# A two-block transformer kernel on one core: the first norm in wide pieces on three engines, parameter rows loaded behind it, the last norm applied while banks are emptied, one weight split moved among norm jobs

## The chip, the cores and the metric

The kernel runs on one core of one Trainium2 chip. The metric is the device time of one execution in microseconds (us), the smaller the better. The kernel before took 2709.87 us (median of 3 runs, 2707.84 to 2711.51).

Engine names in rows: PE is TensorE (matmul), PEld its weight load, DVE is VectorE, ACT is ScalarE, POOL is GpSimd, SP is SyncE. A name with a q behind it (ACTq, SPq, PEq) is the instruction queue of that engine: issuing a DMA is shown there.

## The reference, cut to what matters

Sequence 256, width 1024, two blocks of two layers each, everything in float32. Only the places that the change touches are written out.

```
def rmsnorm(x, g):                         # gain g per column
    return x * rsqrt(mean(x*x, -1) + 1e-6) * g

# block 1, layer 0 begins
h    = rmsnorm(x, g_mix[0])                # the FIRST norm
proj = h @ w_in[0]                         # first weights used: the 512 columns of a_in ("glu")
# ... three attentions, a convolution, gates, w_out, a convolutional FFN; then layer 1

# block 2, layer l: xs (256 rows of latents), cs (256 rows of context), both modulated
xs, cs = ffn_half_step(xs, ..), ffn_half_step(cs, ..)
hx = rmsnorm(xs, mix_norm[l]) * (1 + m1) + m0
hc = rmsnorm(cs, mix_norm[l]) * (1 + n1) + n0
px = hx @ w_in[l]                          # "in": 4 units of 256 columns, then q, kv, k_rope
# in the last layer hc is needed for the kv columns only
# ... latent attention, Fourier mix, convolution, w_out, a second FFN
return rmsnorm(xs, final_norm)             # the LAST norm, behind the last FFN
```

## The kernel before, in words

Activations lie transposed in SBUF: `x[128, 8, 256]` holds chunk c of 128 model columns on the partitions and the 256 tokens along the row. A matrix product is done in float32 quality out of three products of a rounded format: every operand is split into a high part and a rest, and PE computes high·high, rest·high and high·rest (lines 917 to 919). So each weight tile goes through one pipeline, called a *unit* here (up to 128 x 2048 numbers, 1 MB): SP loads it into one of four slots of `raw` (line 761), ACT rounds it into `whi` (`copy`, line 1378), DVE subtracts to get `wlo` (line 1842), and PE runs 48 matmuls of 256 columns per unit. Semaphores count units: `s_raw` landed, `s_hi` rounded, `s_lo` rest ready, `s_acc` matmuls done, `s_accfree` bank emptied. A slot of `raw` is free once the rest of the unit in it is computed. Every engine runs its own list of instructions strictly in the order in which it is written out by hand; there is no scheduler.

A norm over the 1024 columns (`norm_x`) works like this. ACT squares the eight chunks of x into `sq` (line 1424). DVE adds seven of them into `rstd` (lines 1873, 1875). PE multiplies a matrix of ones with that sum and with the eighth square, so that each partition of `stat` holds the sum over all columns (lines 876, 878). DVE transposes `stat` into `root` (line 1885), ACT takes the root of a few columns (`few`, line 1452), DVE inverts them (1893) and spreads them back into `rstd` (1895). Then come *jobs*, one per chunk: DVE writes `hf = x·gain·rstd` (1920), ACT rounds it into `h_hi`, DVE subtracts to get `h_lo` (1905, or 1907 with a bias). The gain is a column of `par`.

**The head.** All small parameters (gains, biases, convolution taps) lie in HBM as rows. 65 small DMAs fetch them into `prow`, every second one issued by ACT (line 1375), the others by POOL (line 800), and PE turns the seven blocks of 128 rows into columns of `par` (line 864, evacuated by ACT, 1378). ACT issues the load of x (1372), of the constant tables (1373) and its half of the rows first, and only then begins to compute: it copies the turned x out of four banks, rounds the first unit, squares. DVE waits for all of `par` before it goes on with the norm (the wait in front of line 2072). PE turns the rows between the norm's sums and the first matmuls of "glu" (`first_units`, 939 to 941).

**"in" of the last layer.** `scale_norm` on DVE runs 16 jobs, the eight of xs first, then the eight of xc. Units 0 and 1 of "in" are used by PE while the jobs of xs are made. ACT rounds unit 2 and DVE makes its rest only after all 16 jobs. A unit's result goes out of its bank by ACT (`fr`, `cb`, `u`), the last one by DVE (line 2335), and the next phase, q01, may begin once all of these banks are emptied.

**The tail.** After the last unit of the last FFN (`down1`, eight units, one per chunk of x), DVE adds the gated result to x (2281), ACT squares it, PE sums, DVE and ACT make `rstd`, DVE makes eight tiles `fin = x·gain·rstd` (1915), PE turns them back in sixteen 128x128 transposes (864), ACT copies four banks into `ostage` (1378), and SP writes 1 MB to HBM in one DMA (791).

## Time and profile before

| | |
|---|---|
| median of 3 runs | 2709.87 us |
| the profiled execution | 2706.84 us |
| its span (first to last instruction) | 2705.0 us |
| PE busy | 2578.7 us, 95% of the span |
| PE weight load busy | 2252.0 us, 83% |
| DVE busy | 1482.9 us, 55% |
| ACT busy | 1035.0 us, 38% |
| POOL busy | 76.4 us, 3% |
| chain that ended last | PE 87%, DVE 6%, ACT 3%, issue 2%, POOL 1%, DVEq 1% |
| mean granted TensorE clock | 0.991 of full |

The span is what the profile sees; the execution's own time is 1.84 us more. "Busy" for PE counts overlapping, pipelined matmuls. The granted clock has two levels here, 1.2 and 2.4 GHz; 0.50 in a window means that the whole window ran at 1.2 GHz.

### The profile page before, as it was taken

What the parts mean: (1) busy time and instruction counts of PE and PEld (TensorE: products, weight loads), DVE (VectorE), ACT (ScalarE), POOL (GpSimd) and SP (SyncE); (2) the same over time, 40 slices, a digit from 0 to 9 for tenths busy, and PEclk for the clock granted to TensorE, in tenths of its full rate; (3) what the DMA queues carried; (4) which work ended last, traced back from release to release, by engine and by line L of the source; (5) the groups of instructions that cost most, each with busy time, mean ns of one, the idle gap of its engine ahead of it and who ended that gap; (6) DMA issues with size and microseconds to landing.
All of it is one profiled execution on the core that took longest, in us unless ns stands there. A gap on an engine that the chain in (4) does not pass through costs nothing.

```text
span 2705.0 us, 47365 instructions
## 1 busy us (share of the span) xinstructions
PE 2578.7 (95%) x19887; PEld 2252.0 (83%) x19887; DVE 1482.9 (55%) x2170; ACT 1035.0 (38%) x1411; POOL 76.4 (3%) x108
## 2 busy tenths in 40 slices
PE   6998999999899999999999999999999999898998
PEld 5998999899889978888776678888788888776998
DVE  4787786787678563333525564333543333546555
ACT  4445464555456432122334432122332222444433
POOL 4003000000200000000000000000000000000000
PEclk9999999999999999999999999999999999999999
DMA  7477765757676552432426542332342433554572
GB/s 207 162 251 165 210 181 161 220 193 228 162 213 172 166 161 80 115 95 74 158 79 196 157 125 79 103 107 72 119 129 75 120 88 92 164 164 132 152 204 91
DMA packets 613576, 393.61 MB, mean 146 GB/s; under 512 B 47804, under 2 KB 609656, under 8 KB 613270
## 3 DMA queue, kind: packets, MB, share of 16 engines
q1 hardware_dynamic: 609552, 383.03, 48.7%
q0 software_dynamic: 2816, 6.53, 1.2%
q8 instruction: 136, 2.23, 0.4%
q10 hardware_dynamic: 1029, 1.47, 0.1%
q14 instruction: 43, 0.34, 0.0%
HBM read 389.94 MB, written 1.05 MB: 145 GB/s over the span
## 4 chain that ended last, share of the span: by engine, by line
PE 87%; DVE 6%; ACT 3%; issue 2%; POOL 1%; DVEq 1%; ACTq 0%; POOLq 0%
PE acc L917 12%; PE acc L918 12%; PE acc L919 12%; PE scores L917 6%; PE scores L918 6%; PE scores L919 6%; PE scores L958 3%; PE scores L960 3%; PE scores L959 3%; PE acc L958 3%; PE acc L960 3%; PE acc L959 3%; DVE wlo L1842 2%; PE stat L1085 2%; ACT whi L1378 1%
## 5 line engine op out<-in xcount | busy, mean ns | idle before, releaser
L1378 ACT ACTIVATE whi<-raw 128x2048 fp32r<-128x2048 f32 (+2 forms) x336 | 567.5, 1690 | 848.1 <-PE acc L919 236.3
L1842 DVE TENSOR_TENSOR wlo<-raw,whi 128x2048 fp32r<-128x2048 f32 (+2 forms) x315 | 653.5, 2075 | 245.4 <-ACT whi L1378 244.9
L917 PE MATMUL acc<-h_hi,whi 128*128 128x256 f32 (+1 forms) x2084 | 671.6, 322 | 19.8 <-DVE x L2217 7.8
L918 PE MATMUL acc<-h_lo,whi 128*128 128x256 f32 (+1 forms) x2084 | 663.3, 318 | 0.0
L919 PE MATMUL acc<-h_hi,wlo 128*128 128x256 f32 (+1 forms) x2084 | 662.6, 318 | 0.0
L917 PEld LDWEIGHTS acc<-h_hi,whi 128*128 128x128 f32 x2084 | 395.7, 190 | 58.1 <-DVE wlo L1842 13.6
L918 PEld LDWEIGHTS acc<-h_lo,whi 128*128 128x128 f32 x2084 | 396.1, 190 | 28.4 <-issue 1.2
L919 PEld LDWEIGHTS acc<-h_hi,wlo 128*128 128x128 f32 x2084 | 396.0, 190 | 27.5
L917 PE MATMUL scores<-h_hi,whi 128*128 128x256 f32 (+1 forms) x928 | 310.6, 335 | 0.1
L918 PE MATMUL scores<-h_lo,whi 128*128 128x256 f32 (+1 forms) x928 | 309.0, 333 | 0.0
L919 PE MATMUL scores<-h_hi,wlo 128*128 128x256 f32 (+1 forms) x928 | 309.0, 333 | 0.0
L917 PEld LDWEIGHTS scores<-h_hi,whi 128*128 128x128 f32 x928 | 174.9, 188 | 20.4 <-issue 1.4
L918 PEld LDWEIGHTS scores<-h_lo,whi 128*128 128x128 f32 x928 | 175.0, 189 | 17.4
L919 PEld LDWEIGHTS scores<-h_hi,wlo 128*128 128x128 f32 x928 | 175.0, 189 | 17.4
L958 PE MATMUL scores<-a_hi,whi 128*128 128x256 f32 (+1 forms) x528 | 177.8, 337 | 4.3 <-DVE wlo L1842 4.3
L958 PE MATMUL acc<-a_hi,whi 128*128 128x256 f32 (+1 forms) x528 | 177.1, 335 | 1.3 <-DVE wlo L1842 1.3
L959 PE MATMUL scores<-a_lo,whi 128*128 128x256 f32 (+1 forms) x528 | 177.4, 336 | 0.0
L960 PE MATMUL scores<-a_hi,wlo 128*128 128x256 f32 (+1 forms) x528 | 177.4, 336 | 0.0
L959 PE MATMUL acc<-a_lo,whi 128*128 128x256 f32 (+1 forms) x528 | 176.8, 335 | 0.0
L960 PE MATMUL acc<-a_hi,wlo 128*128 128x256 f32 (+1 forms) x528 | 176.6, 335 | 0.0
L2306 DVE TENSOR_TENSOR a_hi<-sg,acc 128x512 f32 (+3 forms) x48 | 29.8, 621 | 238.9 <-PE acc L919 238.9
L2306 DVE TENSOR_TENSOR a_hi<-sg,scores 128x512 f32 (+3 forms) x40 | 24.8, 621 | 191.3 <-PE scores L919 191.3
(302 smaller groups left out, 3487.8 us busy)
## 6 DMA issues: line engine op xcount, KB each, us to landing
raw<-in_ffn_w_in_dram SPq DMA_DIRECT2D x176, 512.0 KB, 5.0
raw<-in_w_mod_dram SPq DMA_DIRECT2D x72, 1024.0 KB, 5.2
raw<-in_w_in_dram SPq DMA_DIRECT2D x62, 1024.0 KB, 5.8
raw<-in_w_up_dram SPq DMA_DIRECT2D x88, 512.0 KB, 5.1
raw<-in_ffn_w_out_dram SPq DMA_DIRECT2D x64, 704.0 KB, 4.7
raw<-in_w_down_dram SPq DMA_DIRECT2D x32, 704.0 KB, 4.8
raw<-in_w_out_dram SPq DMA_DIRECT2D x16, 1024.0 KB, 5.9
raw<-in_w_branch_dram SPq DMA_DIRECT2D x16, 512.0 KB, 6.9
```

Source lines behind the costliest of these rows:

```text
L917: pe.matmul(bank, wh, hi[:, c0 + k, 0:width], start=(k == 0), stop=False)
L918: pe.matmul(bank, wh, lo[:, c0 + k, 0:width], start=False, stop=False)
L919: ins = pe.matmul(bank, wl, hi[:, c0 + k, 0:width], start=False, stop=(k == ph.shape[0] - 1))
L958: pe.matmul(bank, wh, hi[:, c0 + k, 0:width], start=(k == 0), stop=False)
L959: pe.matmul(bank, wh, lo[:, c0 + k, 0:width], start=False, stop=False)
L960: ins = pe.matmul(bank, wl, hi[:, c0 + k, 0:width], start=False, stop=(k == FH - 1))
L1085: ins = pe.matmul(to[32 * q:32 * q + 32, :, :], cond[:, c, :], w[:, :, q, :], start=(c == 0), stop=(c == DC - 1))
L1378: return act.activation(out_, in_, ACT.Copy, **kw)
L1842: dve.tensor_tensor(wlo[:, s % 2, 0:el], raw[:, slot, 0:el], f32(whi[:, s % 2, 0:el]), ALU.subtract).then_inc(s_lo, 1)
L2306: dve.tensor_tensor(hi, sg2[:, b, 0:T], bank_of(ph, j, 1, 4)[:, 0:T], ALU.mult).then_inc(s_accfree, 1)
```

## The change

It has three separate parts.

1. *Head.* x is loaded in two halves of 512 KB. ACT issues, beside x and the tables, only the 8 pieces of rows of block 0 (the block in which the gain of the first norm lies). Twelve pieces are issued by POOL, the other 45 by SP, behind the first four weight loads; SP begins its weight loads only when the first half of x has landed. DVE, not ACT, copies the turned x out of the banks. Squares and sums are 512 columns wide (two chunks at once), and PE sums three times instead of twice. The first unit is rounded in halves. The rest of unit 0 is made half by POOL and half by DVE, the rest of unit 1 wholly by POOL. `par` of block 0 is enough for the norm; the other six blocks are turned by PE behind "glu".
2. *"in".* In the last layer the rounding and the rest of units 2 and 3 are put in among the 16 jobs (in front of jobs 9 and 12, counted from 0), with the emptying of units 0 and 1 beside them. In both layers the rounding of the next unit now stands ahead of the emptying of a bank.
3. *Tail.* `fin = x·gain` is made chunk by chunk during the last `down1`, without `rstd`. PE turns it into four banks. The sum of squares is taken per token (four matmuls with 2 columns each), so that 1/rms is a number per partition, and it is multiplied in when ACT and DVE empty the banks. The output leaves in four DMAs of 256 KB.

```diff
+POOL_PIECES = 12
+IN_AMONG = (9, 12)
...
+    first_pieces = [p for p in pieces if p[0] == 0]
+    later_pieces = [p for p in pieces if p[0] > 0]
+    pool_pieces, sp_pieces = later_pieces[:POOL_PIECES], later_pieces[POOL_PIECES:]
+    blocks_turned = [range(1)] + [range(b, min(b + 4, row_blocks)) for b in range(1, row_blocks, 4)]
...
+            sp.wait_ge(s_x, 16)
             for ph in phases:
...
                     if i is None:
+                        if ph.g[j] == RAW:
+                            for b, p0, take, c0, c1, src in sp_pieces:
+                                sp.dma_start(prow[p0:p0 + take, b, c0:c1], src).then_inc(s_prow_sp, 16)
                         slot_free(ph.g[j])
                         load(ph, j, ph.g[j], j)
...
+            for half in range(2):
+                cols = slice(half * 512, half * 512 + 512)
+                for t, done in enumerate((s_tile_act, s_tile_dve)):
+                    sp.wait_ge(done, half + 1)
+                    sp.dma_start(out_rows[:, t, cols], ostage[:, t, cols]).then_inc(s_out, 16)
...
         def _(pool):
...
+            pool.wait_ge(s_head_hi, 1)
+            first_low(0, 0).then_inc(s_head_lo, 1)
+            pool.wait_ge(s_head_hi, 2)
+            first_low(1, 0)
+            pool.wait_ge(s_lo, 1)
+            pool.wait_ge(s_hi, 2)
+            first_low(1, 1).then_inc(s_lo, 1)
...
         def _(pe):
...
+            pe.wait_ge(s_sq, 8)
+            for e in range(2):
+                pe.matmul(stat[:, 0:SEQ], ones, sq[:, 1, e * SEQ:(e + 1) * SEQ], start=(e == 0), stop=False)
+            pe.wait_ge(s_sum, 7)
+            pe.matmul(stat[:, 0:SEQ], ones, rstd[:, 0:SEQ], start=False, stop=True).then_inc(s_sum, 1)
...
+            pe.wait_ge(s_prow_first, 16 * len(first_pieces))
+            turn_rows(blocks_turned[0])
...
                 first_units(nm + "glu", h1_hi, h1_lo, SEQ, 1)
+                if l == 0:
+                    pe.wait_ge(s_prow_pool, 16 * len(pool_pieces))
+                    pe.wait_ge(s_prow_sp, 16 * len(sp_pieces))
+                    for blocks in blocks_turned[1:]:
+                        turn_rows(blocks)
...
         def _(act):
...
-            for c in range(0, DC, 2):
-                turned(x[:, c:c + 2, :])
-            act.wait_ge(s_raw[0], 16)
-            copy(whi[:, 0, 0:phases[0].el], raw[:, 0, 0:phases[0].el]).then_inc(s_hi, 1)
...
-            for b in range(0, row_blocks, 4):
-                turned(par[:, b * P:min((b + 4) * P, n_rows)])
...
             for c in range(0, DC, 2):
+                k = n("turn", 1)
+                act.wait_ge(s_turned, k)
+                if c >= 4:
+                    act.wait_ge(s_sum, c - 2)
+                act.activation(sq[:, (k - 1) % 2, :].rearrange("p (a b) -> p a b", a=2), x[:, c:c + 2, :],
+                               ACT.Square).then_inc(s_sq, 2)
+                if c == 2:
+                    first_high(0, 0)
+            n("sum", 8)
+            turned_rows(blocks_turned[0])
+            first_high(0, 1)
+            first_high(1, 0)
+            take_root(norm_x(1, ("g_mix", 0), h1_hi, h1_lo))
+            first_high(1, 1)
...
+                def among(e):
+
+                    if e == IN_AMONG[0]:
+                        round_next(nm + "in", 1, None)
+                        in_out(0)
+                    if e == IN_AMONG[1]:
+                        round_next(nm + "in", 2, None)
+                        in_out(1)
...
+                round_norm(norm_mod(l, 1, 2), among if last else None)
...
+                round_next(nm + "in", 3, None)
+                in_out(2)
...
         def _(dve):
...
+            for c in range(0, DC, 2):
+                k = c // 2 + 1
+                dve.wait_ge(s_turn, k)
+                dve.tensor_copy(x[:, c:c + 2, :], (ptp, op_[:, :])[k % 2].rearrange("p (a b) -> p a b", a=2)).then_inc(s_turned, 1)
...
+            dve.wait_ge(s_hi, 1)
+            dve.wait_ge(s_head_lo, 1)
+            dve.tensor_tensor(wlo[:, 0, half:2 * half], raw[:, 0, half:2 * half], f32(whi[:, 0, half:2 * half]),
                               ALU.subtract).then_inc(s_lo, 1)
...
-            dve.wait_ge(s_turned, 4 + row_turns)
...
+            dve.wait_ge(s_turned, 5)
...
+                            if h == 1 and after_ph is None:
+                                settle()
+                                dve.tensor_scalar(fin[:, j, :], x[:, j, :], pcol("final", j), None, ALU.mult).then_inc(s_fin, 1)
...
-            scale_norm(norm_final())
+            dve.wait_ge(s_tokroot, 1)
+            dve.reciprocal(inv[:, 0:4], few[:, 0:4]).then_inc(s_tokinv, 1)
+            settle()
+            for half in range(2):
+                dve.wait_ge(s_fturn, 4 * half + 4)
+                dve.tensor_scalar(ostage[:, 1, half * 512:half * 512 + 512], final_bank(1, half), inv[:, 2:3], None,
+                                  ALU.mult).then_inc(s_tile_dve, 1)
```

Three places in the instruction lists, as the two programs have them. First ACT from its first instruction to the root of the first norm. Before (the rows between the two DMAs of parameters are left out):

```order
L1372 DMA stage<-in_x_dram 128x2x1024
L1373 DMA shared<-tables_dram 128x384
...
L1375 DMA prow<-in_final_norm_dram 8x128
L1378 ACT_TABLE_LOAD
L1378 ACTIVATE x<-op 128x512
L1378 ACTIVATE x<-turns 128x512
L1378 ACTIVATE x<-op 128x512
L1378 ACTIVATE x<-turns 128x512
L1378 ACTIVATE whi<-raw 128x2048
L1424 ACTIVATE sq<-x 128x256 x7
L1378 ACTIVATE whi<-raw 128x1024
```

Now:

```order
L1441 DMA stage<-in_x_dram 128x2x512
L1442 DMA shared<-tables_dram 128x384
L1443 DMA stage<-in_x_dram 128x2x512
...
L1445 DMA prow<-in_ffn_conv_w_dram 12x128
L1504 ACT_TABLE_LOAD
L1504 ACTIVATE warm<-eps 128x1
L1652 ACTIVATE sq<-x 128x512 x2
L1448 ACTIVATE whi<-raw 128x1024
L1652 ACTIVATE sq<-x 128x512 x2
L1448 ACTIVATE par<-op 128x128
L1448 ACTIVATE whi<-raw 128x1024 x2
L1522 ACTIVATE few<-root,eps 128x8
```

The copies of x are gone from ACT, the squares are four instead of eight and of twice the width, the rounding of the first weights stands in halves between and behind them, and the copy of one block of `par` stands in front of the root.

Second, DVE in the last layer of block 2 at "in" (`hf<-xc` and `h_lo` are the jobs of the context rows; `wlo<-raw,whi` is the rest of a unit). Before, from the eighth job of xc on:

```order
L1920 SCALAR_TENSOR_TENSOR hf<-xc,mod_gs,rstd 128x256
L1907 SCALAR_TENSOR_TENSOR h_lo<-hf,mods,h_hi 128x256 x2
L2031 STREAM_TRANSPOSE mod_t<-stat 128x192
L2039 TENSOR_TENSOR mods<-mod_t,par 128x12
L1842 TENSOR_TENSOR wlo<-raw,whi 128x2048 x3
L2335 TENSOR_TENSOR u<-scores,u 128x256 x2
```

Now, from the second job of xc on (jobs 10, 11, 13 and 14 left out):

```order
L1954 TENSOR_TENSOR wlo<-raw,whi 128x2048
L2034 SCALAR_TENSOR_TENSOR hf<-xc,mod_gs,rstd 128x256
L2019 SCALAR_TENSOR_TENSOR h_lo<-hf,mods,h_hi 128x256
...
L1954 TENSOR_TENSOR wlo<-raw,whi 128x2048
L2034 SCALAR_TENSOR_TENSOR hf<-xc,mod_gs,rstd 128x256
L2019 SCALAR_TENSOR_TENSOR h_lo<-hf,mods,h_hi 128x256
...
L2034 SCALAR_TENSOR_TENSOR hf<-xc,mod_gs,rstd 128x256
L2019 SCALAR_TENSOR_TENSOR h_lo<-hf,mods,h_hi 128x256 x2
L2145 STREAM_TRANSPOSE mod_t<-stat 128x192
L2153 TENSOR_TENSOR mods<-mod_t,par 128x12
L1954 TENSOR_TENSOR wlo<-raw,whi 128x2048
L2478 TENSOR_TENSOR u<-scores,u 128x256 x2
```

Two of the three rests behind the jobs (those of units 2 and 3) have moved in among them; the third (q01's) has stayed.

Third, PE behind the last matmul of the last FFN. Before:

```order
L960 MATMUL acc<-a_hi,wlo 128x256
L876 MATMUL stat<-rstd,shared 128x256
L878 MATMUL stat<-sq,shared 128x256
L864 MATMUL op<-shared,fin 128x128 x4
L864 MATMUL turns<-shared,fin 128x128 x4
L864 MATMUL op<-shared,fin 128x128 x4
L864 MATMUL turns<-shared,fin 128x128 x4
```

Now (five more pairs like the first two rows behind the last matmul are left out):

```order
L997 MATMUL acc<-a_hi,wlo 128x256
L1420 MATMUL turns<-shared,fin 128x128
L1420 MATMUL scores<-shared,fin 128x128
...
L1430 MATMUL stat<-shared,rstd 128x2
L1431 MATMUL stat<-shared,sq 128x2
L1430 MATMUL stat<-shared,rstd 128x2
L1431 MATMUL stat<-shared,sq 128x2
L1420 MATMUL turns<-shared,fin 128x128
L1420 MATMUL scores<-shared,fin 128x128
L1420 MATMUL turns<-shared,fin 128x128
L1420 MATMUL scores<-shared,fin 128x128
```

Twelve of the sixteen transposes stand ahead of the sums now, and none of them needs `rstd`.

## Rows read from the trace of the kernel before

**Rows 1.** PE's waits over the span: waited for, us, times, longest.
```profile
PE stat L876 <- DVE rstd L1875: 12.8, 6, 8.3
PE op L864 <- DMA shared<-tables_dram: 8.5, 1, 8.5
```

**Rows 2.** Timeline of the head: start us, us, instruction [idle before <-releaser].
```profile
0.75 0.51 ACTq L1372 DMA_DIRECT2D stage<-in_x_dram  x1
13.59 0.32 ACTq L1375 DMA_DIRECT2D prow<-in_final_norm_dram  x1
20.18 0.71 ACT L1424 ACTIVATE sq<-x 128x256 f32<-128x256 f32 x2
25.42 1.04 ACT L1378 ACTIVATE whi<-raw 128x1024 fp32r<-128x1024 f32 x1
26.15 1.22 PE L876 MATMUL stat<-rstd,shared 128*128 128x256 f32 x2 [8.30 <-DVE rstd L1875]
26.49 1.23 DVE L1860 TENSOR_TENSOR wlo<-raw,whi 128x1024 fp32r<-128x1024 f32 x1 [0.40 <-ACT whi L1378]
28.26 0.45 DVE L1885 STREAM_TRANSPOSE root<-stat 128x256 f32<-128x256 f32 x1 [0.55 <-PE stat L878]
30.08 0.31 ACT L1452 ACTIVATE few<-root,eps 128x8 f32<-128x8 f32 x1
31.41 0.20 DVE L1893 RECIPROCAL inv<-few 128x8 f32<-128x8 f32 x1
33.73 0.55 PE L939 MATMUL acc<-h_hi,whi 128*128 128x256 f32 x1 [4.12 <-issue]
```

**Rows 3.** DMA issues of the first 1.2 us: size, us from issue to landing.
```profile
stage<-in_x_dram ACTq DMA_DIRECT2D x1, 1024.0 KB, 6.7
raw<-in_w_in_dram SPq DMA_DIRECT2D x1, 1024.0 KB, 9.4
```

**Rows 4.** Timeline of SP's queue, the fourth weight load.
```profile
6.27 3.95 SPq L761 DMA_DIRECT2D raw<-in_w_in_dram  x1
```

**Rows 5.** Timeline behind "glu": its last banks, then the rest of nak.
```profile
46.79 0.73 ACT L1584 ACTIVATE y<-scores 128x256 f32<-128x256 f32 x2 [0.73 <-PE scores L941]
51.09 2.29 DVE L1842 TENSOR_TENSOR wlo<-raw,whi 128x2048 fp32r<-128x2048 f32 x1 [2.77 <-ACT whi L1378]
```

**Rows 6.** DVE and POOL working at once (timeline), and POOL's group (busy us, mean ns).
```profile
245.23 3.50 DVE L1842 TENSOR_TENSOR wlo<-raw,whi 128x2048 fp32r<-128x2048 f32 x1
L834 POOL TENSOR_TENSOR gates<-gates 128x1024 f32<-128x1024 f32 x8 | 19.1, 2412 | 634.4 <-DVE gates L2202 634.4
```

**Rows 7.** Timeline of "in" in the last layer.
```profile
2327.28 21.82 SPq L761 DMA_DIRECT2D raw<-in_w_in_dram  x9
2331.75 0.48 DVE L1920 SCALAR_TENSOR_TENSOR hf<-xc,mod_gs,rstd 128x256 f32<-128x256 f32 x1
2338.19 1.89 ACT L1378 ACTIVATE whi<-raw 128x2048 fp32r<-128x2048 f32 x1
2342.46 0.58 PE L917 MATMUL acc<-h_hi,whi 128*128 128x256 f32 x1 [4.16 <-DVE wlo L1842]
2356.72 0.43 DVE L2335 TENSOR_TENSOR u<-scores,u 128x256 f32<-128x256 f32 x1 [0.91 <-PE scores L919]
```

**Rows 8.** Windows of "in": length, PE busy (matmuls), granted clock, DMA share, GB/s.
```profile
2344.00:2348.00 4.00, 4.00 (x21) 0.50 1.07 303
2352.00:2356.00 4.00, 4.00 (x36) 1.00 0.00 0
```

**Rows 9.** Timeline of the tail: the last chunk of x, the last copy.
```profile
2689.67 0.48 DVE L2281 SCALAR_TENSOR_TENSOR x<-acc,mod_gates,x 128x256 f32<-128x256 f32 x1 [2.50 <-PE acc L960]
2700.02 0.60 ACT L1378 ACTIVATE ostage<-turns 128x512 f32<-128x512 f32 x1
```

**Rows 10.** The output's DMA: size, us to landing.
```profile
out_dram<-ostage SPq DMA_DIRECT2D x1, 1024.0 KB, 4.0
```

**Rows 11.** Transposes at full clock, by tile: ns min/median/max, first and last start.
```profile
L864 PE MATMUL op<-shared,cstage x8: 272/273/273, 886.0 to 922.1; 128*128 128x128 f32 x8
L864 PE MATMUL turns<-shared,cstage x8: 272/272/273, 886.4 to 922.5; 128*128 128x128 f32 x8
```

More of the change, by code:

```diff
@@ L641, in norm_final @@
         def norm_final():
-            return dict(chunks=[[(x[:, c, :], 0, SEQ)] for c in range(DC)], width=SEQ, mat=ones, scale=1.0 / D,
-                        jobs=[(x[:, c, :], 0, SEQ, pcol("final", c), None, fin[:, c, :], None) for c in range(DC)])
+            return dict(chunks=[[(x[:, c, :], 0, SEQ)] for c in range(DC)], width=SEQ)
         def pairs_block1(l):
@@ L1913, in scale_norm @@
                         rest_second(second, 1)
+                    if between:
+                        between(e)
                     if lo is None:
@@ L2326, in _ @@
                 ph = by_name[nm + "in"]
-                for j in range(4):
-                    rest_ahead(nm + "in", j, None)
+                for j in range(3 if last else 1, 4):
+                    rest_next(nm + "in", j, None)
                 for m in range(2):
```

170 lines of the change are left out of this document (116 added, 54 removed).

## The prediction

> **What bounds the kernel now.** I read the list of PE's waits over the whole span first: PE is busy nearly all the time, so only its idle stretches and what the change puts into its list can move the end. The longest are DVE's sums of squares (12.8 us, 8.3 at once) and the first load (8.5), both in the head [rows 1]. Then the timeline of the head [rows 2]: ACT issues DMAs until 13.9 us, before it computes anything; the squares run from 20.2, DVE inverts the root at 31.4 and PE's first product of "glu" begins at 33.73. From there PE is busy: the head is a serial piece, and what it gets shorter comes off the end unless "glu" or the phases behind it stall. Third, the only long stall inside that the change touches: "in" of the last layer, where PE waits 4.16 us for the rest of unit 2 [rows 7], and works at 1.2 GHz afterwards, 21 matmuls in 4 us instead of 36 [rows 8]. Last the tail: the last matmul ends at 2689.64 (0.03 before DVE adds it to x), the last copy at 2700.62 [rows 9], and the output lands 4.0 us after its issue [rows 10]; the span ends at 2705.0, 15.4 us behind the last matmul.
>
> **The head, step by step.** *Start.* 512 KB instead of 1 MB, alone in the queues: 1 MB of x landed in 6.7 us beside a weight load [rows 3]. The output's 4.0 us for 1 MB alone [rows 10] is the nearer row for an undisturbed transfer, and half of it should be nearer 3.5; so x at 4.3, and the tables, issued 0.6 later, at 5. PE's turns, DVE's copies (new there, about the 0.60 of ACT's copy of the same size [rows 9]) and the first squares are done by 9. Then ACT waits for unit 0, in order: its load now starts when x has landed, at 4.4. The first load took 9.4 with x's megabyte ahead [rows 3]; without it I take 5.3, so R = 9.7 (from 8.4, at the output's 4.0, to 13.8, at 9.4).
>
> *From R to "glu".* Rounding half of the unit 1.04; two squares of 512 columns, each like two of 256, 0.71, together 1.3 (0.63 each); three sums on PE instead of two, 1.22 for the first and 0.9 for each more, 3.0; turning block 0, 0.5; its copy, 0.3; half a unit rounded, 1.04; DVE's half of the rest, 1.23; root's transpose 0.45; root 0.31 [rows 2]. Sum 9.2, with some 0.1 of hand-over at each of nine places 9.9; from the reciprocal to PE's first product 2.3 as before (31.41 to 33.73). ACT's second rounding of 1.04 lies beside DVE's rest. That gives R + 12.2 less 0.9, since the squares' last add and DVE's sum lie beside PE's first two sums and PE's clock may be up by then: R + 11.3 = 21.0.
>
> *What POOL costs.* POOL makes 1024 columns in 2.41 us; and while it worked, DVE's rest of 2048 columns took 3.50 us instead of 2.29 [rows 5, 6]. So the part speaks against itself a little: POOL's second and third pieces, 17 to 22 us, lie beside DVE's rest, its `hf` and its `h_lo`. At half as much again on 1.2 us of rest and on the first two jobs I add 0.7. "glu" starts at 21.7, against 33.73: 12.0 less. POOL's last piece is done at about 22.5, and PE needs it in the seventh step, at 1.28 us a step (six matmuls of 0.21) after 29: covered, and still if a piece took 4.8. The Trainium skill (GPSIMD Engine Reference, Key points) says that GpSimd shares its SBUF interfaces with VectorE and contends with VectorE instructions that have two SBUF inputs. By that rule the rest and the jobs are slowed and the copies out of banks are not, which is what the 3.50 shows; without the rule and the row the sum would be 0.7 better.
>
> *What comes back behind "glu".* Seven transposes and two copies of `par` now stand there. Before, ACT's last bank of "glu" was begun at 46.79, and DVE's rest of nak ended at 53.38, which PE awaited [rows 5]. PE turns at 0.12 us each, 0.9 (at 0.23, as it did cold, 1.6), ACT copies the second bank some 1.0 to 1.4 us later than it would have begun its next work, and nak is later by that: +1.1. The rows must have landed. SP issues 45 pieces behind four weight loads. The fourth of these held SP for 3.95 us, until 10.2 [rows 4]; it now starts 3.7 later, so until 13. ACT issued its 33 pieces at 0.37 us each (1.9 to 13.9): 45 of them end at 30, landed at 33, and "glu" ends at 21.7 + 13 = 34.7. Covered by 1.7. The fifth weight load goes out at 30 instead of 22.6, lands by 36, and its unit is rounded at about 48: covered. Head: 12.0 − 1.1 = 10.9 (range 5 to 14).
>
> **"in" of the last layer.** Seven jobs take 6.44 us (from `hf` at 2331.75 to the rounding at 2338.19), 0.92 each. The load of unit 2 is issued at 2327.28 [rows 7]; with 6.2 us to landing it is there at 2333.5 (at x's 6.7, 2334.0). ACT rounds until 2335.4, DVE makes the rest until 2337.7, and PE ends unit 1 at 2338.3 (its wait of 4.16 ends at 2342.46): no stall. Job 9 starts at 2337.7 instead of 2331.75, job 12 2.8 later; unit 3 is rounded at 2340.2 to 2342.1, its rest ends at 2344.4. PE: unit 2 takes 5.7 us at full clock (48 matmuls, 36 in 4.0 us and a bit more [rows 8]) until 2344.0, unit 3 until 2350.1. DVE has four jobs left, ACT then rounds q01's weights at 2348.1 to 2350.0, DVE ends the rest at 2352.3, empties two banks (0.43 each), and q01 begins at 2353.2. Before it began behind the 2356.72 + 0.43, at 2357.2: 4.0 less. But PE now idles 3.1 us there, and after the idle 4.16 the clock was at its lower level, from 2342.5 to 2348.0 at least, where 15 of 36 matmuls are lost [rows 8]: 5.5 × 15/36 = 2.3. I give that an even chance: −1.2, so 2.8 net (range 1 to 5). The reordering in layer 0 moves a copy of 1 us behind a rounding for which nobody waits: 0.
>
> **The tail.** `fin` is a DVE instruction of at most 0.48 in each step of `down1`, between two rests with some 1 us of idle between: hidden; if not, 8 × 0.4 = 3. With L the last matmul: twelve transposes at 0.12 are 1.4 us ([rows 11] show a group of four beginning 0.4 after the other); the square of the last chunk is ready at L + 1.0, beside them. Four products of 2 columns are not shown by any row; at one loaded 128x128 each in two passes I take 0.25 each, 1.0 (between 0.3 and 2.4, the price of a 256-column sum each). Root 0.3, reciprocal 0.2, with hand-overs L + 3.3; two copies of 0.60 per engine, 4.5; the first DMA goes out at L + 4.0, the last at 5.2. The 4.0 us of 1 MB are about 1.2 fixed and 2.8 of data, so the four end at L + 8.0 with the end of the program. 15.4 − 8.0 = 7.4 (range 5 to 8.5). The Trainium skill (DMA: Bandwidth & Descriptors, "Anatomy of one DMA") gives about 2.0 us fixed per DMA plus the bytes' time, which speaks against four small ones. By it the last piece would take 2.6 and the first three would lie ahead of it, so the end would be at L + 8.2; the row's 4.0 for 1 MB has less of fixed cost.
>
> **Sum.** 10.9 + 2.8 + 7.4 = 21.1 off the profiled execution: span 2705.0 to 2683.9, and 2706.84 to 2685.7. The median shown is 3.0 above that execution, so the forecast for a median is 2709.87 − 21 = 2689 us, 0.8% less.
>
> **The rivals.**
> 1. *The head gives half.* ACT takes its work strictly in order: two squares stand behind the first weights. If unit 0 lands as late as before counted from its issue (9.4, so at 13.8), "glu" starts 4.1 later; likewise if the rows on SP land late (POOL needs 0.5 per piece: 45 × 0.5 ends at 35.5, landed at 38.5, PE waits 3.8). For it: the only such load measured took 9.4. Against: it had x's megabyte ahead. Head 6 instead of 10.9: 2694.
> 2. *"in" gives nothing.* The idle time moves from unit 2 to q01, and the clock falls there as it did before; if the load of unit 2 lands late too, jobs and rest shift with it. Saves 0 to 1: 2691. It would be told by a low clock behind 2353.
> 3. *More than the sum.* R at 8.4 and POOL's pieces free: 2 less in the head, no fall of the clock 1.2, and an earlier output: 2685.
> 4. *Slower: the rows on SP.* PE waits behind "glu" for all 45 pieces, and each goes through a queue that weight loads fill. The fourth load shows SP held for 3.95 us by one issue. If pieces are held in the same way, each one's price p decides: they land at 16 + 45p, PE needs them at 34.7, so the head's 10.9 are gone from p = 0.66 on, and the whole gain of 21 from p = 0.88; at p = 1.0 the time is 2715. For it: the 3.95. Against: ACT's 33 pieces of the same form at 0.37, beside the same loads.
>
> **Chances.** Forecast (gain 17 to 25) 0.58, rival 1 0.18, rival 2 0.10, rival 3 0.10, rival 4 0.04, most of which ends above 2700. The range that leaves out 2 in 10 or less goes from 2682 to 2698. About 0.2%, 5.4 us, is what a measurement of this kernel can tell from no change. Faster by more than that: all but rival 4 and a bad pile-up of 1 and 2, 0.94; within it 0.03; slower 0.03.
>
> **What would show it.** First product of "glu" at 20 to 24 us, with ACT's rounding of unit 0 as the last thing awaited before the last two squares; PE's wait for parameter rows behind "glu" under 1 us; nak begun about 7.8 us behind the end of "glu", not 6.7; in "in" no wait of PE in front of units 2 and 3 and one of about 3 us in front of q01; last matmul to end of span about 8 us. The prediction is wrong if PE waits for rows or for POOL's rest, if the time between 60 and 2300 us changes by more than 3 us, or if the tail takes over 10.

## The result and the profile after

The changed kernel takes 2688.7 us (median of 4 runs, 2686.24 to 2689.63); the kernel before took 2708.86 us in the same comparison. The ratio is 0.9923, 95% interval 0.9911 to 0.9934. The profiled execution took 2686.24 us with a span of 2684.4, 20.6 less than the 2705.0 before. The forecast was 2689, with 21.1 off the span: the time is right. Two of the three terms behind it are not, and they cancel.

To see where the time went I use one event that both programs have 28 times, the start of ACT's root of a norm (`few`). Each row of the table is such a start, or the end of the span; a number is how much earlier (minus) or later it stands than in the kernel before. Between two rows the difference of two numbers is what that stretch gained.

| before, us | what lies ahead of it | changed | head alone | "in" alone | tail alone |
|---|---|---|---|---|---|
| 63.50 | the head, "glu" and the rows behind it | -7.41 | -6.30 | +0.31 | +0.54 |
| 491.79 | layer 0 of block 1 | -8.21 | -6.99 | +4.01 | +4.89 |
| 2320.90 | all up to "in" of the last layer | -8.12 | -7.31 | +3.78 | +5.15 |
| 2382.85 | "in" | -13.93 | -8.96 | -0.25 | +5.27 |
| 2493.39 | attention and mixing of the last layer | -13.29 | -8.30 | -0.27 | +5.22 |
| 2705.0 (end) | last FFN and the tail | -20.6 | -8.3 | +0.2 | -2.2 |

So the changed kernel gained 7.4 in the head, 0.7 on the way to "in", 5.8 in "in" (predicted 2.8), lost 0.6 behind it, and gained 7.3 in the tail (predicted 7.4).

**The head after**, timeline (start us, us, instruction, idle before it); it answers to [rows 2]:

```profile
4.94 6.97 SPq L778 DMA_DIRECT2D raw<-in_w_in_dram  x4
11.87 1.06 ACT L1448 ACTIVATE whi<-raw 128x1024 fp32r<-128x1024 f32 x1 [2.80 <-DMA raw<-in_w_in_dram]
13.01 2.34 POOL L831 TENSOR_TENSOR wlo<-raw,whi 128x1024 fp32r<-128x1024 f32 x1 [5.62 <-ACT whi L1448]
16.47 1.22 PE L1148 MATMUL stat<-rstd,shared 128*128 128x256 f32 x2 [0.38 <-DVE rstd L2189]
20.19 4.92 POOL L831 TENSOR_TENSOR wlo<-raw,whi 128x1024 fp32r<-128x1024 f32 x2 [4.84 <-ACT whi L1448]
20.87 0.31 ACT L1522 ACTIVATE few<-root,eps 128x8 f32<-128x8 f32 x1 [0.77 <-DVE root L1997]
22.11 3.28 DVE L2034 SCALAR_TENSOR_TENSOR hf<-x,par,rstd 128x256 f32<-128x256 f32 x2
25.82 0.55 PE L976 MATMUL acc<-h_hi,whi 128*128 128x256 f32 x1 [7.92 <-DVE h_lo L2017]
46.01 0.38 PE L954 MATMUL acc<-h_hi,whi 128*128 128x256 f32 x1 [1.00 <-DVE wlo L1954]
```

"glu" begins at 25.82 instead of 33.73: 7.9 earlier, where 12.0 was predicted. ACT gets unit 0 at 11.87, not 9.7. Two `hf` take 3.28 us, which before were under 0.5 each. The last row is the first product of nak behind "glu"; it was at 53.43, so 7.4 is what was left, and the rows cost 0.5 instead of 1.1. No wait of PE for parameter rows is in the list of waits.

DVE's groups of that stretch by shape (busy us, mean ns, idle before):

```profile
L2034 DVE SCALAR_TENSOR_TENSOR hf<-x,par,rstd 128x256 f32<-128x256 f32 x3 | 3.8, 1280 | 0.1
L2187 DVE TENSOR_TENSOR rstd<-rstd,sq 128x512 f32<-128x512 f32 x1 | 2.4, 2353 | 2.7 <-ACT sq L1652 2.7
```

**"in" after**, timeline, DVE and PE (answers to [rows 7]), then windows (to [rows 8]):

```profile
2326.92 2.29 DVE L1954 TENSOR_TENSOR wlo<-raw,whi 128x2048 fp32r<-128x2048 f32 x1 [3.60 <-ACT whi L1448]
2333.83 2.29 DVE L1954 TENSOR_TENSOR wlo<-raw,whi 128x2048 fp32r<-128x2048 f32 x1 [1.99 <-ACT whi L1448]
2336.17 0.39 PE L954 MATMUL scores<-h_hi,whi 128*128 128x256 f32 x1 [0.50 <-DVE wlo L1954]
2344.86 0.39 PE L954 MATMUL acc<-h_hi,whi 128*128 128x256 f32 x1 [2.67 <-DVE u L2478]
```

```profile
2340.00:2344.00 4.00, 2.19 (x19) 1.99 (x17) 3.15 (x5) 3.21 (x4) 0.00 (x0) 1.00 0.09 14
2344.00:2348.00 4.00, 3.14 (x26) 3.14 (x27) 1.83 (x3) 0.00 (x0) 0.00 (x0) 1.00 0.67 132
2356.00:2360.00 4.00, 4.00 (x19) 3.25 (x19) 0.56 (x1) 0.00 (x0) 0.00 (x0) 1.00 0.87 271
```

PE waits 2.67 us in front of q01 (about 3 was predicted) and 0.50 in front of unit 3, and the granted clock (the third number from the end) stays at 1.00. q01 begins at 2344.86 instead of 2357.20, 12.3 earlier; less the 8.1 brought along, 4.2. The other 1.6 come right behind: the kernel before had a window at 2368 to 2372 with a granted clock of 0.57, and the changed one has 1.00 in the corresponding one (last row). That these 1.6 are the change's is not shown. The kernel with the head alone has the old "in", with the old waits; its q01 begins at 2349.84, 7.4 earlier, which is what it had brought along, and at the mark behind it is 9.0 ahead. It too lacks the low window. The two windows, before and with the head alone:

```profile
2368.00:2372.00 4.00, 4.00 (x11) 3.15 (x12) 0.90 (x1) 0.07 (x1) 0.00 (x0) 0.57 0.77 251
2360.00:2364.00 4.00, 3.50 (x15) 2.92 (x16) 1.54 (x2) 0.70 (x3) 0.00 (x0) 1.00 0.62 202
```

**The tail after**, timeline (answers to [rows 9]), and the output's DMAs (to [rows 10]):

```profile
2676.18 0.48 DVE L2416 SCALAR_TENSOR_TENSOR x<-acc,mod_gates,x 128x256 f32<-128x256 f32 x1 [2.37 <-PE acc L997]
2677.29 0.33 PE L1430 MATMUL stat<-shared,rstd 128*128 128x2 f32 x2
2678.32 0.26 ACT L1930 ACTIVATE few<-stat,eps 128x4 f32<-128x4 f32 x1 [1.21 <-PE stat L1431]
2678.89 1.41 DVE L2578 TENSOR_SCALAR ostage<-scores,inv 128x512 f32<-128x512 f32 x2
2679.54 1.83 SPq L816 DMA_DIRECT2D out_dram<-ostage  x4
```

```profile
out_dram<-ostage SPq DMA_DIRECT2D x4, 256.0 KB, 2.5
```

From DVE's last sum (2676.18) to the end of the span are 8.2 us; before it was 15.3.

### The profile page after: what moved, and what is told of

It reads as the page before. It is cut to its first block, busy times and chain, and to the rows that moved or that the text cites. A ratio compares the mean times of both kernels' runs of the same rounds, so it can differ in the third digit from the quotient of the medians.

```text
span 2684.4 us, 47388 instructions
## 1 busy us (share of the span) xinstructions
PE 2571.2 (96%) x19893; PEld 2245.8 (84%) x19893; DVE 1485.0 (55%) x2169; ACT 1029.4 (38%) x1403; POOL 73.7 (3%) x91
## 3 DMA queue, kind: packets, MB, share of 16 engines
HBM read 389.94 MB, written 1.05 MB: 146 GB/s over the span
## 4 chain that ended last, share of the span: by engine, by line
PE 86%; DVE 6%; ACT 3%; issue 2%; POOL 1%; DMA 1%; DVEq 1%; ACTq 0%; SPq 0%; POOLq 0%
PE acc L954 12%; PE acc L955 12%; PE acc L956 12%; PE scores L954 6%; PE scores L956 6%; PE scores L955 6%; PE scores L995 3%; PE scores L997 3%; PE scores L996 3%; PE acc L995 3%; PE acc L997 3%; PE acc L996 3%; DVE wlo L1954 2%; PE stat L1122 2%; ACT whi L1448 2%
## 5 line engine op out<-in xcount | busy, mean ns | idle before, releaser
L1448 ACT ACTIVATE whi<-raw 128x2048 fp32r<-128x2048 f32 (+3 forms) x337 | 567.5, 1685 | 858.8 <-PE acc L956 244.6
```

The source lines that it names most:

```text
L1448: return act.activation(out_, in_, ACT.Copy, **kw)
```

## The experiments

**1. Each part alone.** The kernel before, with the head, "in" or the tail of the changed kernel and nothing else. The edits are the corresponding parts of the diff.

> Only the head part of the change, on the kernel before; "in" and tail are the old ones. The theory read from the trace of the changed kernel: 'glu' begins near 25.8 us, 7.9 earlier than the 33.7 before, and the time falls by 8 us (7 to 9). The prediction's own term was 10.9, with 'glu' at 21.7. If the head's gain in the changed kernel depended on the other parts (through where the granted clock falls), the time would fall by less than 6 or by more than 10. PE should again wait about 1.0 us for the rest of nak behind 'glu', and DVE's sum of 512 columns beside POOL's piece should again take over 2 us.

> Only the 'in' part, on the kernel before. The theory read from the trace of the changed kernel: 4.3 us less up to the first product of q01 and 1.1 more because the granted clock no longer falls in the windows that stood at 2340 to 2348 and 2368 to 2372 before; together 5.4 (4 to 6). The prediction's term was 2.8: 4.0 less 1.2 for an even chance of a fallen clock. The rival, that the idle time only moves and the clock falls in front of q01 as it fell at unit 2, gives 1 to 2 us. In the trace: granted clock 1.00 in all windows of 4 us from unit 2 to q01, or a fall there.

> Only the tail part, on the kernel before. Theory: the end of the span lies 8.2 us behind the last product of down1 instead of 15.4, so 7.1 to 7.4 us less; nothing earlier in the program moves. Rival: making fin in each step of down1 (eight DVE instructions of 0.35 us) delays the rests there, and the gain is 1 to 3 us smaller; PE would then show new waits for DVE in the last down1.

Measured against the kernel before at 2708.05 us:

| kernel | median, us | ratio | 95% interval |
|---|---|---|---|
| head alone | 2701.37 | 0.9973 | 0.9963 to 0.9983 |
| "in" alone | 2704.57 | 0.9987 | 0.9978 to 0.9996 |
| tail alone | 2700.95 | 0.9974 | 0.9964 to 0.9983 |

That is 7.3, 3.5 and 7.0 us off by the ratios, 17.8 in sum, against 20.9 for the three together; each interval is some 2.5 us wide on either side, so the sum doesn't contradict it, and doesn't prove that nothing is shared. In the traces (table above) the tail gave 7.4 and the head 6.3 at the first mark. The head's unit 0 landed 1.1 later there (ACT began it at 12.95). "in" gained 4.0 between its marks, not 5.8, since the clock fell in this trace behind PE's wait in front of q01:

```profile
2352.00:2356.00 4.00, 2.37 (x20) 2.17 (x19) 3.11 (x4) 3.40 (x4) 0.00 (x0) 1.00 0.09 14
2356.00:2360.00 4.00, 2.95 (x19) 2.95 (x20) 2.02 (x4) 0.00 (x0) 0.00 (x0) 0.83 0.64 125
2360.00:2364.00 4.00, 4.00 (x28) 4.00 (x27) 0.00 (x0) 0.38 (x1) 0.00 (x0) 0.75 0.96 289
```

The wait is as long as in the changed kernel (2.68 us against 2.67), so the length of the wait does not decide it. Of the nine kernels here with this order in "in" (those with the later places of experiment 5 left out), the clock fell right behind that wait in two, this one and r_first (0.61 in its window at 2352), which gained 4.0 and 4.3; the other seven gained 5.8 to 5.9. By these the even chance given to a fall was rather high, and 1.8 us hang on it (5.8 less 4.0). The traces of "in" alone and of the tail alone are moreover 3.7 and 4.4 us longer between the marks at 107 and 492, where their programs do the same as before. Nothing was edited there, so that is a spread between executions, and the reason why stretches are compared here, not only times.

**2. POOL's part of the first rests.** In the changed kernel DVE makes all of it instead:

```diff
-            pool.wait_ge(s_head_hi, 1)
-            first_low(0, 0).then_inc(s_head_lo, 1)
...
+            first_low(0, 0)                      # DVE, behind its last sum
+            first_low(0, 1).then_inc(s_lo, 1)
...
+                if e == 3:
+                    first_low(1, 0)
+                if e == 5:
+                    first_low(1, 1).then_inc(s_lo, 1)
```

> The changed kernel with POOL's three pieces of the first two units' rests given to DVE: both halves of unit 0 in front of the root's transpose, the halves of unit 1 among the jobs of the first norm (in front of jobs 3 and 5). Theory (POOL's two-input instructions hold up DVE's): the sum of 512 columns takes 0.7 us instead of 2.35, the third sum on PE begins 1.6 earlier, the second hf takes 0.5 instead of 2.8, and 'glu' begins at 22 us instead of 25.8; PE then waits 1 to 2 us for DVE inside 'glu', since 2.5 us of rests lie among the jobs. Net 1.5 to 3 us less than the changed kernel. Rival (the long DVE instructions have another cause, such as the DMA traffic of the head): they stay over 2 us without POOL, 'glu' begins later than 25.8, since DVE has 3.6 us more to do, and the time is 1 to 3 us more.

Measured: 2692.95 us, ratio 0.9944 (0.9931 to 0.9958), 4 to 6 us slower than the changed kernel. The sum took 0.69 us, as the theory says, but ACT could round unit 1 only here:

```profile
9.13 9.85 POOL L848 DMA_DIRECT2D rpb<-in_na_rpb_dram  x16
26.32 1.06 ACT L1435 ACTIVATE whi<-raw 128x1024 fp32r<-128x1024 f32 x1 [7.15 <-DMA raw<-in_w_in_dram]
```

POOL's waits for the first rests had also kept its own next loads back, 1.2 MB of tables and sixteen pieces of 64 KB; without them these went out from 7.4 us on, ahead of unit 1. The experiment had changed two things. With one line more, the loads are held again:

```diff
+            pool.wait_ge(s_lo, 2)
             for l in range(DEPTH):
                 pool.dma_start(sink[:, l, :], ...)
```

> As the run without POOL's pieces, but POOL issues its next loads (sink, the tables of block 1, the bias rows) only once the rests of units 0 and 1 are ready, about where they were issued in the changed kernel. Theory: what undid the gain there were these loads, issued from 7.4 us on instead of 25, which made unit 1 land at 26.3; with the gate unit 1 is there by 18 us, 'glu' begins at 22 to 23 (25.8 in the changed kernel), PE waits 1 to 2 us inside 'glu' for jobs behind DVE's rests, and the time is 1 to 3 us less than the changed kernel. Rival: the rests on DVE cost as much as POOL's contention did; 'glu' begins at 22 to 23, but its end and the time stay where they are, within 1 us.

Measured: 2689.81 us, 0.9920 (0.9907 to 0.9934), the same as the changed kernel. DVE's groups between 12 and 23 us, and PE's first product of "glu":

```profile
L2022 DVE SCALAR_TENSOR_TENSOR hf<-x,par,rstd 128x256 f32<-128x256 f32 x3 | 1.4, 482 | 0.1
L2175 DVE TENSOR_TENSOR rstd<-rstd,sq 128x512 f32<-128x512 f32 x1 | 0.7, 693 | 2.5 <-ACT sq L1640 2.5
```

```profile
22.54 0.55 PE L964 MATMUL acc<-h_hi,whi 128*128 128x256 f32 x1 [5.70 <-DVE h_lo L2005]
```

So POOL's pieces cost 3.3 us ahead of "glu" (25.82 to 22.54, of which 0.3 is an earlier landing of unit 0), although DVE now does POOL's work as well. Behind "glu" the product of nak is 1.8 earlier (44.18), PE having waited 0.8 more inside. At the mark at 82.83 us the gain over the changed kernel was 1.2, and then it went away in places that nobody had touched: 0.5 by 492, and 4.4 between 2392.69 and 2493.39, where its granted clock was low around 2450; the changed kernel lost 0.7 there.

**3. POOL in small pieces.**

```diff
+                for a in range(part * half, part * half + half, 256):
+                    cols = slice(a, a + 256)
+                    ins = pool.tensor_tensor(wlo[:, j, cols], raw[:, j, cols], f32(whi[:, j, cols]), ALU.subtract)
+                return ins
```

> The changed kernel, POOL's pieces of 1024 columns cut into four of 256 each (0.6 us by size). If a DVE instruction with two SBUF inputs is held until the POOL instruction beside it ends, the DVE sum of 512 columns takes 0.7 to 1.4 us instead of 2.35 and the second hf under 1.2 instead of 2.8, and 'glu' begins 2 to 3 us earlier. If the two only share bandwidth in proportion, or if POOL's next piece takes over at once, both stay over 2 us and nothing changes (within 0.5 us, or up to 0.5 later by the overhead of nine more instructions).

Measured: 2687.16 us, 0.9922 (0.9908 to 0.9936): not to be told from the changed kernel. In the trace, with unit 0 landing 0.6 later, "glu" begins 1.55 earlier, the mark at 82.83 is 0.9 earlier and the span 1.3 shorter (2683.1). DVE and POOL side by side:

```profile
14.15 0.73 DVE L2189 TENSOR_TENSOR rstd<-rstd,sq 128x512 f32<-128x512 f32 x1 [3.25 <-ACT sq L1654]
19.96 6.53 POOL L832 TENSOR_TENSOR wlo<-raw,whi 128x256 fp32r<-128x256 f32 x8 [2.95 <-ACT whi L1450]
24.20 0.83 DVE L2036 SCALAR_TENSOR_TENSOR hf<-x,par,rstd 128x256 f32<-128x256 f32 x1
24.96 0.95 DVE L2019 TENSOR_TENSOR h_lo<-hf,h_hi 128x256 fp32r<-128x256 f32 x1
```

In this trace a DVE instruction waits for the POOL instruction under way and then passes. The changed kernel shows it better; `hf` by tile (ns min/median/max, first and last start) and POOL's third piece:

```profile
L2034 DVE SCALAR_TENSOR_TENSOR hf<-x,par,rstd x2: 796/1677/2558, 22.1 to 22.8; 128x256 f32<-128x256 f32 x2
22.59 2.52 POOL L831 TENSOR_TENSOR wlo<-raw,whi 128x1024 fp32r<-128x1024 f32 x1
```

In the changed kernel POOL's second and third pieces end at 22.59 and 25.11; the two `hf`, begun at 22.11 and 22.83, took 0.80 and 2.56 us and ended at 22.9 and 25.4, 0.3 behind each. By proportional sharing neither would end with POOL's piece. The Trainium skill says so (Trainium Architecture — The Big Picture, "What this means for kernel authors"): between VectorE and GpSimd the shared port pair is held by one at a time, an exclusive lock and no split of bandwidth. These two traces agree; experiment 7 has an instruction that does not fit so simply.

**4. When unit 0 lands.** Three edits of SP's order in the changed kernel: the wait for x behind the first weight load, no such wait, and a wait for unit 0's landing ahead of the load of unit 1.

```diff
-            sp.wait_ge(s_x, 16)                       # all three but the last
...
+                        if ph.g[j] == 1:
+                            sp.wait_ge(s_x, 16)       # r_first
+                            sp.wait_ge(s_raw[0], 16)  # r_alone, which keeps the wait for x
```

> The changed kernel with the wait for x moved behind the first weight load: unit 0's load goes out at 0.7 us beside x, the other three when x has landed. Theory: ACT gets unit 0 by 8 to 9 us instead of 11.84, x lands 1 to 1.5 us later (6 instead of 4.9) since 1.5 MB share the queues; the last squares are then set by the turned x, not by unit 0, and 'glu' begins 1 to 2 us earlier, so does the end. Rival: x as late as in the kernel before (7.4) or later, everything behind it moves back, and 'glu' begins no earlier than 25.8.

> The changed kernel without the wait for x ahead of the weight loads: all four go out from 0.7 us on. Theory: x shares the queues with 4 MB of weights and lands at 7 to 8 us instead of 4.9, its second half at 8 to 9, unit 0 at 9 to 10; the squares end no earlier than now, 'glu' begins within 1 us of 25.8 and the time stays within 1 us. Rival: the wait for x only delays unit 0, and without it 'glu' begins 2 us earlier.

> The changed kernel with SP holding the loads of units 1 to 3 until unit 0 has landed. Theory: unit 0 takes 6.9 us to land (6.7 to 8.1 in other traces) because 3 MB issued right behind it share the queues; alone it lands 4.0 to 4.5 us after its issue at 4.9, so ACT begins to round it at 9 to 9.5 instead of 11.84, the third sum and 'glu' come 2 us earlier (near 23.8), and PE behind 'glu' 2 us earlier too. The price: the rows on SP begin near 16 instead of 12 and end near 34, against a need at the end of 'glu' near 36: PE may wait up to 2 us for them, and a gain of 0 to 2 us is left. Rival: the landing does not depend on what is issued behind it (it is set by x's second half and the rows ahead); ACT begins to round at 11.5 to 12 as before, and the later rows make it 1 to 2 us slower.

| kernel | median, us | ratio (95%) | mark at 63.50 |
|---|---|---|---|
| r_first | 2693.19 | 0.9936 (0.9922 to 0.9949) | -3.86 |
| r_free | 2692.78 | 0.9936 (0.9923 to 0.9950) | -4.11 |
| r_alone | 2689.33 | 0.9922 (0.9909 to 0.9936) | -6.57 |
| changed | 2688.7 | 0.9923 (0.9911 to 0.9934) | -7.41 |

All three theories fell. Beside x (r_first) unit 0 took 10.0 us and x's first half 6.1 instead of 4.2; PE's first turn of x came 2.8 later (8.42 instead of 5.64), and "glu" 2.4 later. So the wait for x is worth 2.4 us at "glu", more than I had thought. At the first mark it is 3.3 to 3.6, but about 1 of that arises inside "glu", where PE ran slower for longer (28 products between 32 and 36 us in r_first and 31 in r_free, 36 in the changed kernel). And alone (r_alone) unit 0 took 7.0, as with three more loads behind it (6.9). "glu" begins at 25.84, as in the changed kernel. The 0.84 us that r_alone is behind at the mark are not the rows' either, which are landed when "glu" ends: PE ran 25 products of "glu" between 28 and 32 us instead of 32, with a granted clock shown as 1.00 in both traces. Windows of r_alone (the last three numbers are granted clock, DMA share, GB/s):

```profile
2.00:4.00 2.00, 0.00 (x0) 0.00 (x0) 0.00 (x0) 0.00 (x0) 2.00 (x5) 1.00 0.81 220
4.00:6.00 2.00, 0.59 (x3) 0.59 (x4) 0.00 (x0) 0.79 (x1) 2.00 (x6) 1.00 1.02 380
6.00:8.00 2.00, 1.98 (x10) 1.61 (x9) 1.27 (x2) 1.33 (x3) 1.39 (x3) 1.00 1.16 273
8.00:10.00 2.00, 1.34 (x7) 0.86 (x5) 1.90 (x5) 0.63 (x1) 0.00 (x0) 1.00 0.94 256
10.00:12.00 2.00, 0.00 (x0) 0.00 (x0) 0.60 (x2) 0.12 (x1) 0.00 (x0) 1.00 0.26 83
```

What has been moved until it lands is 2.4 MB (220 + 380 + 273 + 256 + 83 and 11 before, times 2 us): unit 0 (1.05), both halves of x (1.05), the tables (0.2) and the first rows. The DMA engines are busy from 2.5 us on. What lies *ahead* of unit 0, in all queues, sets R, not what SP issues behind it. The Trainium skill (DMA: Bandwidth & Descriptors, "Queues, rings and completion order") says that each engine takes the descriptors of one issuer's ring in order; by that, later loads of SP can't delay unit 0, and the run agrees. I had not weighed it. The 273 and 256 GB/s between 6 and 10 us (276 in both windows in the changed kernel), with a share of about 1, against 380 before, made me think of the small packets of the rows. Experiment 7 moves POOL's rows away.

**5. "in" with later places.**

```diff
-IN_AMONG = (9, 12)
+IN_AMONG = (12, 15)
```

> The changed kernel with the roundings and rests of units 2 and 3 of 'in' in front of jobs 12 and 15 instead of 9 and 12. In its trace DVE stands idle for 3.60 us and 1.99 us in front of the two rests, since ACT may round only when PE is done with the unit that holds the buffer; three jobs of 0.92 us fit into each gap. Theory: the rests stay where they are (2326.9 and 2333.8), the last jobs are made 1.8 to 2.7 us earlier, PE's wait in front of q01 falls from 2.7 to about 1 us, and the mark behind 'in' comes 1.5 to 2 us earlier. Rival: the freed time only moves the clock's fall (a shorter wait changes nothing, and the next idle stretch is hit), or job 12 delays the rest of unit 2 and PE waits there; then the mark moves by less than 0.5 us.

Measured: 2687.48 us, 0.9920 (0.9906 to 0.9933). Between the marks around "in" 6.89 us are gained instead of 5.81, so 1.1 more, of 1.5 to 2 expected; the kernel of experiment 7, with the same places, gains 6.85. PE's waits there:

```profile
PE scores L954 <- DVE wlo L1954: 0.9, 1, 0.9
PE acc L954 <- DVE u L2478: 0.5, 1, 0.5
PE acc L954 <- DVE wlo L1954: 0.5, 1, 0.5
```

The 2.67 in front of q01 has become 0.5, but 0.5 and 0.4 more are waited in front of units 2 and 3 (0.48 and 0.89 instead of 0 and 0.50). The theory had the rests stay where they are; counted from the mark in front of "in", they came 1.1 later, since ACT, in its order, rounds unit 2 only behind the last `h_hi` of the jobs put in front of it (at 2326.91, with that `h_hi` begun at 2326.49). Behind it, 2.2 us are lost between 2392.69 and 2493.39 instead of 0.7: in this trace the window at 2452 has a clock of 0.62.

**6. One output DMA.**

```diff
+            sp.wait_ge(s_tile_act, 2)
+            sp.wait_ge(s_tile_dve, 2)
+            sp.dma_start(out_rows, ostage[:, :, :]).then_inc(s_out, 16)
```

> The changed kernel with one output DMA of 1 MB behind all four copies instead of four of 256 KB. Only the trace is of use, as the difference is far below what a time can show. Theory by the kernel before (4.0 us for the same 1 MB): issued some 0.9 us behind the first of the four, landed 4.0 later, the span ends 0.2 to 0.6 us later after the last product of down1 than the 8.3 of the changed kernel. Rival, by which every DMA has a fixed part of about 2 us and the small ones overlap it: 1 us later or more.

One execution, 2688.59 us. Its DMA takes the 4.0 us of [rows 10] again. From the mark at 2493.39 to the end it gains 6.9, where the other kernels with the new tail gain 7.1 to 7.4: by this one trace splitting is worth 0.2 to 0.5 us, and the rival's 1 us or more is out.

**7. Three edits at once.** Small pieces, later places in "in", and POOL's rows behind its first rest:

```diff
             first_low(0, 0).then_inc(s_head_lo, 1)
+            for b, p0, take, c0, c1, src in pool_pieces:
+                pool.dma_start(prow[p0:p0 + take, b, c0:c1], src).then_inc(s_prow_pool, 16)
             pool.wait_ge(s_head_hi, 2)
```

> Three edits on the changed kernel at once: POOL's rests in pieces of 256 columns; 'in' with its roundings and rests in front of jobs 12 and 15; and POOL's twelve row pieces issued behind its first rest instead of at the start, since unit 0 waits for some 2.4 MB in all (x, tables, rows, the unit itself), and from 6 to 10 us, while the row pieces' small packets are in the queues, these move 276 GB/s instead of 370. Theory: unit 0 is rounded at 11.0 to 11.5 us instead of 11.84; the mark of the norm behind 'glu' comes 0.9 to 1.5 us earlier by the small pieces and as much as 0.5 by the rows; the mark behind 'in' 1.1 more; the span comes out 2 to 3 us shorter than the changed kernel's 2684.4, unless the granted clock falls once more than there (each fall of the later program cost 1.5 to 4 us), which decides whether the median, 2685 to 2687, can be told from 2688.7. Rival: unit 0's landing has nothing to do with the row pieces (11.8 to 12.6 as in the other traces), and POOL's pieces for unit 1, now 1.4 us later, are awaited by PE inside 'glu': no gain over the small pieces alone.

Measured: 2689.28 us, 0.9926 (0.9912 to 0.9939): no better than the changed kernel, the span is 2687.0. The rows' part came true: ACT begins unit 0 at 10.61 instead of 11.87 (11.56 to 12.95 in the eight other traces that let x go first), and between 6 and 10 us the queues moved 324 and 355 GB/s:

```profile
6.00:8.00 2.00, 1.98 (x10) 1.61 (x9) 1.29 (x2) 1.28 (x3) 0.00 (x0) 1.00 1.05 324
8.00:10.00 2.00, 1.33 (x7) 0.85 (x5) 1.90 (x5) 0.63 (x1) 0.00 (x0) 1.00 1.06 355
```

That the small packets as such are the reason is not shown, and two counts speak against it: between 8 and 10 us the changed kernel had only 28 packets under 512 B in the queues and moved 276 GB/s, while r_free had 232 of them and moved 362. What it is about POOL's rows that slows unit 0 stays open, and that it is they rests on this one trace.

The root came 2.0 earlier. Then all of it was lost at one instruction (`hf` by tile: ns min/median/max; then POOL's pieces and PE, timeline):

```profile
L2036 DVE SCALAR_TENSOR_TENSOR hf<-x,par,rstd x4: 484/870/4675, 20.1 to 27.7; 128x256 f32<-128x256 f32 x4
```

```profile
21.21 5.84 POOL L830 TENSOR_TENSOR wlo<-raw,whi 128x256 fp32r<-128x256 f32 x8
26.58 0.55 PE L978 MATMUL acc<-h_hi,whi 128*128 128x256 f32 x1 [10.68 <-DVE h_lo L2019]
```

One `hf` was held for 4.68 us, through six of POOL's eight pieces, which here ran at 0.72 us each with nothing between them; in the run with small pieces alone their median was 0.90, and DVE got in between. In the trace it began at 20.94 (it ends at 25.62), 0.3 before POOL's first piece at 21.21, so "waits for the one under way and then passes" does not describe it. Whether small pieces let DVE through thus depends on how the two meet; what decides it I can't say from these two traces. "glu" began at 26.58, later than in the changed kernel.

## Why the prediction was right, and where it was wrong

- **The landing of unit 0 (R), in the head.** Predicted 9.7, measured 11.87. Its load went out at 4.94 instead of 4.4 and took 6.9 us instead of 5.3. I had taken "x's megabyte" to be out of the way, and forgot that x's second half, the tables and the rows were still ahead of it, 2.4 MB with the unit itself. ACT began to round it at 10.6 to 13.0 in the traces of all these kernels that let x go first; rival 1 had named this place. Of the miss of 3.5 in the head this is 2.2.
- **POOL's price, in the head.** Predicted 0.7, measured about 3. I read in [rows 6] that DVE's rest took 3.50 us instead of 2.29 and made it "half as much again". I did not put POOL's own row of that moment beside it, two instructions of 1024 columns:

```profile
241.81 4.77 POOL L834 TENSOR_TENSOR gates<-gates 128x1024 f32<-128x1024 f32 x2 [199.82 <-DVE gates L2202]
```

  They end at 246.58. DVE's rest of 2.29 began in effect only there (246.58 + 2.29 = 248.87; it ended at 248.73). A hold reads like a slowdown when one looks at durations and not at ends. Its size is what is left of POOL's instruction, not a share of DVE's. It also struck elsewhere than I had charged it: DVE's rest at 19.19 took its 1.23 us, as POOL's second piece began only at 20.19; the sum of squares, which I had not charged, was held for 1.7, and counted from R the root came 0.75 later than with DVE alone; the other 2.2 came with the two `hf`.
- **From R to "glu".** Predicted R + 11.3 without POOL. With DVE alone it was 11.0 (11.56 to 22.54), so this chain was right in sum; with POOL it was 14.0. (Its nine hand-overs of 0.1 on 9.2 make 10.1, where the working has 9.9.)
- **What comes back behind "glu".** Predicted 1.1, measured 0.5 (from 7.9 to 7.4). The rows on SP were never waited for: rival 4 is out.
- **"in", the order.** Predicted 4.0, measured 4.2, with the wait in front of q01 at 2.67 against 3.1. That PE would not wait in front of unit 3 contradicted the prediction's own times (the rest ready at 2344.4, PE there at 2344.0); 0.50 was measured.
- **"in", the clock.** Predicted -1.2 as a mean over an even chance; here it did not fall, and the low window at 2368 of the kernel before, which I had not counted, was gone too. So +1.6. This part is luck as far as the runs show: the same 1.6 came with the head alone, where "in" is the old one. The sum had a term that was no mean of a size but a coin; the run of "in" alone shows the other side of it, 1.8 us less.
- **The tail.** Predicted 7.4, measured 7.3 and in the nine other kernels that have the new tail with four DMAs 7.1 to 7.4. The end was at 8.2 behind the last sum (8.0 predicted). The four matmuls of 2 columns, which no row had shown, took 0.2 us each from start to start; 0.25 was taken. The first DMA went out 3.4 us behind the last product instead of 4.0, and the transfers took longer than the working had them. Its split of the 4.0 us into 1.2 fixed and 2.8 of data rests on no row; the four pieces landed 2.1 us (the first) to 2.8 us (the last) after their issues, and an estimate from the first of these (2.1 for 256 KB) and the 4.0 for 1 MB is 1.5 fixed and 2.5 of data. The section of the Trainium skill that the prediction quotes (DMA: Bandwidth & Descriptors, "Anatomy of one DMA") states its 2.0 us for DMAs issued by GpSimd; this output is issued by SP. Its formula would give 4.4 and 2.6 us, where 4.0 and 2.1 to 2.8 were measured.
- **The sum.** Head 7.4 and 0.7 on the way instead of 10.9 (-2.8), "in" 5.8 instead of 2.8 (+3.0), 0.6 lost behind it, tail -0.1: 20.6 instead of 21.1. A right total made of two misses of three microseconds that happened to cancel; it was the range, not the working, that covered it. One of the prediction's own signs said so at once: "glu" was to begin at 20 to 24 us, and began at 25.82.

What stays open: whether the 0.7 gained between the head and "in" are the change's, since the traces spread by more than that between the same marks, and why the clock falls in one kernel's last layer and not in another's.

## What to carry to other kernels

When two engines that share a port meet in the trace, compare the *end* of one with the end of the other: if they coincide, the one is held until the other's instruction ends, and giving work to the idle engine can cost the busy one that whole length. When a load is to land early, add up the bytes that are ahead of it in all queues; the loads behind it on the same queue did not matter here (7.0 us without them, 6.9 with). When a stretch gains more than its edit explains, look at the same stretch in a variant that doesn't have the edit. Before you take an instruction away, look at what is queued behind its wait: here it also kept 2.2 MB of other loads out of the critical transfer.

## What was not expected of the hardware

- POOL's 1024-column subtractions (2.34 and 2.52 us) lengthened DVE's sum of 512 columns from 0.69 to 2.35 us and one `hf` from 0.48 to 2.56; a chain of short POOL instructions held another for 4.68.
- DVE's products with one operand in a bank (`gates` from `gates` and a bank, 0.42 us in the kernel before at 243 to 245 us, beside POOL, and 0.41 at 248.65 without it) were not held.
- Between 6 and 10 us the queues moved 273 and 256 GB/s (r_alone) or 276 and 276 (changed) at a DMA share of about 1 while POOL's rows were in them, 324 and 355 without POOL's rows. The packets' size does not explain it (28 under 512 B at 276 GB/s, 232 at 362).
- In the changed kernel PE's products of 256 columns begin 0.21 us apart until 28.95 us and 0.12 apart from 29.13 on, with a granted clock shown as 1.00 in the windows on both sides. In the head the granted clock of the profile does not tell PE's pace.
- The stretch between the marks at 2392.69 and 2493.39, the same program in all, took as long as before in two kernels, 0.65 to 0.7 us longer in five, and 2.1 to 4.8 in six others, which all have windows of lowered granted clock between 2444 and 2464. PE stands there again and again for 0.7 to 1.1 us. A gain of 1 us in the head of this kernel can therefore not be shown by its time.
